# Role preparation of an RWKV-7 branch: the order of the key's factor against the gate copy, and of the norm's sums against the gate product

## The reference

```
r, k, v, wd, ad, gd = jnp.split(p, RWKV_SPLITS, axis=-1)
w_log = -jax.nn.softplus(-(w0 + jnp.tanh(wd) @ w_up)) - 0.5
decay = jnp.exp(-jnp.exp(w_log.astype(f32)))
a = jax.nn.sigmoid(a0 + ad @ a_up)
g = jax.nn.sigmoid(gd) @ g_up
kk = heads(k * k_k)
kk = kk / jnp.maximum(jnp.linalg.norm(kk, axis=-1, keepdims=True), 1e-12)
k = k * (1 + (a - 1) * k_a)
...
bonus = jnp.sum(r_h * k_h * r_k.astype(f32), axis=-1, keepdims=True) * v_h
```

## Time and profile before

| what | value |
|---|---|
| device time, three runs | 3651.9, 3652.07 and 3658.56 us, median 3652.07 |
| the profiled execution | 3661.2 us, its span 3659.3 us |
| busy over the whole span | PE 3353.8 us (92%), DVE 1444.1 (39%), ACT 994.7 (27%), POOL 121.3 (3%) |
| mean granted TensorE clock | 0.954 |

### The profile page before, as it was taken

How to read it: one execution, slowest core, us unless ns; L and a number is a source line. 1 busy time by engine, 2 the same in 40 slices (tenths; PEclk the granted TensorE clock), 3 DMA queues, 4 the chain that set the end, 5 groups by cost and what they waited for, 6 DMA issues and landing times. The chain is left out here.

```text
span 3659.3 us, 70478 instructions
## 1 busy us (share of the span) xinstructions
PE 3353.8 (92%) x28510; PEld 3114.1 (85%) x28510; DVE 1444.1 (39%) x2550; ACT 994.7 (27%) x1542; POOL 121.3 (3%) x126
## 2 busy tenths in 40 slices
PE   6999999999666888869979989999999999699898
PEld 5999999999545777769968789999999999588687
DVE  6566642222483666654435442222222222210433
ACT  5211123333472444431123331111111111211211
POOL 0000000000001222200000000000000000000000
PEclk8999999999776999979989989999999999899999
DMA  5233333433573343333334311111111110411433
GB/s 148 92 125 110 121 132 118 132 124 114 186 273 77 87 94 89 83 138 112 118 130 132 100 58 46 46 46 46 46 46 46 46 46 24 137 47 47 132 116 100
DMA packets 297472, 357.70 MB, mean 98 GB/s; under 512 B 133248, under 2 KB 245760, under 8 KB 285872
## 3 DMA queue, kind: packets, MB, share of 16 engines
q1 hardware_dynamic: 297392, 356.59, 30.8%
HBM read 221.52 MB, written 135.00 MB: 97 GB/s over the span
## 5 line engine op out<-in xcount | busy, mean ns | idle before, releaser
L2295 PE MATMUL psum<-h_hi,up_w_hi 128*128 128x344 f32 x2112 | 675.8, 320 | 15.3 <-DVE up_w_lo L2339 15.3
L2295 PE MATMUL psum<-h_lo,up_w_hi 128*128 128x344 f32 x2112 | 676.7, 320 | 0.0
L2295 PE MATMUL psum<-h_hi,up_w_lo 128*128 128x344 f32 x2112 | 674.4, 319 | 0.0
L434 PE MATMUL psum<-x_hi,proj_w_hi 128*128 128x344 f32 x1632 | 535.7, 328 | 8.5 <-DVE proj_w_lo L521 8.1
L434 PE MATMUL psum<-x_lo,proj_w_hi 128*128 128x344 f32 x1632 | 525.5, 322 | 0.0
L434 PE MATMUL psum<-x_hi,proj_w_lo 128*128 128x344 f32 x1632 | 524.3, 321 | 0.0
L2295 PEld LDWEIGHTS psum<-h_hi,up_w_hi 128*128 128x128 f32 x2112 | 397.5, 188 | 15.3 <-issue 15.3
L2295 PEld LDWEIGHTS psum<-h_hi,up_w_lo 128*128 128x128 f32 x2112 | 397.8, 188 | 0.0
L2295 PEld LDWEIGHTS psum<-h_lo,up_w_hi 128*128 128x128 f32 x2112 | 397.2, 188 | 0.0
L434 PEld LDWEIGHTS psum<-x_hi,proj_w_hi 128*128 128x128 f32 x1632 | 310.0, 190 | 10.3 <-issue 8.2
L2089 PE MATMUL psum<-down_w_hi,down_a_hi 128*128 128x512 f32 x704 | 278.8, 396 | 41.2 <-DVE down_w_lo L2209 30.6
(11 more groups left out here) (296 smaller groups left out, 5152.9 us busy)
## 6 DMA issues: line engine op xcount, KB each, us to landing
up_weight<-in_w_up_tiles SPq DMA_DIRECT2D x22, 1024.0 KB, 4.8
scratch_hidden<-up_hidden SPq DMA_DIRECT2D x22, 1024.0 KB, 3.9
down_a_raw<-scratch_hidden SPq DMA_DIRECT2D x32, 704.0 KB, 5.0
proj_area<-scratch_s_tab SPq DMA_DIRECT2D x32, 608.5 KB, 3.8
scratch_s_tab<-proj_area SPq DMA_DIRECT2D x16, 1089.0 KB, 4.3
proj_weight<-in_w_in_tiles SPq DMA_DIRECT2D x34, 512.0 KB, 4.1
scratch_gates<-proj_mixed SPq DMA_DIRECT2D x16, 1032.0 KB, 4.0
chunk_pre<-scratch_roles SPq DMA_DIRECT2D x128, 128.0 KB, 2.7
```

The lines of the kernel that those rows point to most:

```text
L434: mm = nc.tensor.matmul(psum[:, bank(v, n), 0:N_TOK], w[:, v, k, :], x[:, k, cols], start=(k == 0 and w is w_hi and x is x_hi), stop=(k == ...
L2295: mm = nc.tensor.matmul(psum[:, bank(u, part, n), 0:N_TOK], w[:, u, part, k, :], y[:, k, block_cols(n)], start=(k == 0 and w is w_hi and y ...
```

## The change

Two orders are exchanged. In TensorE's `early`, "norm" with its two waits now stands ahead of "g" with its wait. In ScalarE's `first_steps`, the factor with its two waits now stands ahead of the gate copy with its waits. No instruction is added or removed, and no buffer or semaphore is changed.

```diff
@@ early, TensorE
                 product("a", ups[64:128, 0, c], low[64:128, 0, t], n, a_summed)
-                pe.wait_ge(sig_ready, s + 1)
-                product("g", ups[:, 1, c], low[:, 1, t], n, g_summed)
                 pe.wait_ge(a_ready, s + 1)
                 pe.wait_ge(kk_squared, s + 1)
                 product("norm", heads[:], work[:, h], n, norm_summed)
+                pe.wait_ge(sig_ready, s + 1)
+                product("g", ups[:, 1, c], low[:, 1, t], n, g_summed)
@@ first_steps, ScalarE
                 A.activation(blocks(a[:, slot, 0:n]), banks_of("a", n), ACT.Sigmoid, ...).then_inc(a_ready, 1)
+                act.wait_ge(a_ready, s + 1)
+                if s >= SLOTS_3:
+                    act.wait_ge(bonus_stored[slot], 16 * (s // SLOTS_3))
+                A.activation(bonus[:, slot, 0:n], a[:, slot, 0:n], ACT.Identity, ...).then_inc(factor_ready, 1)
                 act.wait_ge(g_summed, s + 1)
                 if s >= 2:
                     act.wait_ge(gate_stored[h], 16 * (s // 2))
                 A.activation(blocks(gate[:, h, 0:n]), banks_of("g", n), ACT.Copy).then_inc(gate_ready, 1)
-                act.wait_ge(a_ready, s + 1)
-                if s >= SLOTS_3:
-                    act.wait_ge(bonus_stored[slot], 16 * (s // SLOTS_3))
-                A.activation(bonus[:, slot, 0:n], a[:, slot, 0:n], ACT.Identity, ...).then_inc(factor_ready, 1)
```

More of the change, by code:

```diff
@@ L901, in first_steps @@
                 A.activation(blocks(a[:, slot, 0:n]), banks_of("a", n), ACT.Sigmoid, bias=col("a0", j)).then_inc(a_ready, 1)
+                act.wait_ge(a_ready, s + 1)
+                if s >= SLOTS_3:
+                    act.wait_ge(bonus_stored[slot], 16 * (s // SLOTS_3))
+                A.activation(bonus[:, slot, 0:n], a[:, slot, 0:n], ACT.Identity, scale=col("k_a", j), bias=one_less[:, j:j + 1]).then_inc(factor_ready, 1)
                 act.wait_ge(g_summed, s + 1)
@@ L905, in first_steps @@
                 A.activation(blocks(gate[:, h, 0:n]), banks_of("g", n), ACT.Copy).then_inc(gate_ready, 1)
-                act.wait_ge(a_ready, s + 1)
-                if s >= SLOTS_3:
-                    act.wait_ge(bonus_stored[slot], 16 * (s // SLOTS_3))
-                A.activation(bonus[:, slot, 0:n], a[:, slot, 0:n], ACT.Identity, scale=col("k_a", j), bias=one_less[:, j:j + 1]).then_inc(factor_ready, 1)
             A.preload_act_table_set("sigmoid_and_others")
```

## The result

The changed kernel is slower: 3679.9 us in the median of five runs (3673.41 to 3684.64) against 3652.99 for the kernel before (five runs, 3651.9 to 3658.56). The ratio is 1.0072, with an interval of 1.0057 to 1.0087. That is +26.9 us between the medians, where +28.4 was forecast.

The account below looks back on a forecast made before the run. It took VectorE as nearest to a bound in role preparation, which passes its changes to the end. Six loops at +22.9 us and the first two units at +5.5 gave +28.4, 3680.5 us on 3652.07; range 3664 to 3690.

Parts of the forecast that it names:

- The factor's gain: VectorE's waits for the key's factor before L955, 3.69 and 4.00 us in units 3 and 5, would go.
- The series as the loop: From one L978 to the next, TensorE's and ScalarE's series bounds every unit: 19.98 us, +22.9 us over six loops.
- The clock: TensorE idles about 5 us; "a" and "norm" start at 1.2 GHz; the rise comes 4.5 us after "norm" begins.
- The head: First two units, before the first L978: a later gate copy costs +5.5 us, bounds +5.0 and +7.6.
- VectorE past unit 6: Past L978 of unit 6 no product of `early` is left and VectorE alone sets the pace: 0.
- Rival 1: Steady work raises TensorE's clock during "a"; "norm" and "g" run fast: +14.2 us, 3666.3; chance 0.12.
- Rival 2: TensorE's clock never falls, all loops 16.35 us: +4.0 us, 3656.1; chance 0.07.
- Rival 3: "norm" and "g" end early enough to hide ScalarE's exponentials; VectorE's factor waits go: −7.7 us, 3644.4; chance 0.06.
- Rival 4: Time gained at the factor and lost at the gate copy cancel: 3652 us; chance 0.02.
- rival 5: All loops with TensorE's products at 1.2 GHz: +37.6 us, 3689.7; chance 0.05.

Follow-up runs that it names:

- the second pair: Kernel before and changed kernel, each unaltered and run once more for its trace: 3648.2 and 3684.4 us.
- e7: Changed kernel with the gate product computed twice in a row: 3691.4 us (one run).
- e8: Changed kernel with the gate copy moved behind the exponentials (unit 0's stays) and the gate product computed twice: 3642.2 us (one run).
- e4: Changed kernel with the gate copy moved behind the previous unit's exponentials, unit 0's staying in place: 3644.5 us, ratio 0.9963 to the kernel before.
- e5: Changed kernel with more unread filler matmuls in TensorE's idle stretches than the first filler kernel had: 3656.5 us, ratio 0.9987 to the kernel before.
- e3: Changed kernel with matmuls whose sums nobody reads, filling TensorE's idle stretches: 3671.3 us, ratio 1.0029 to the kernel before.

## Why the prediction was right

The mechanism held, and the sum did too: +28.4 forecast, +26.9 measured. That the sum came so close is in part luck. In the first pair of traces the loops gave 24.9 us for 22.9, the head 2.7 for 5.5 and the end −0.6 for 0, and these misses cancel; the second pair has 24.7, 6.1 and 0, 30.9 in all. Part by part:

- *The factor's gain.* The waits before L955 fell from 15.7 to 1.7 us, as put. Nothing of it reached the end, since those units now wait further on. The wait for the norm's sums at L957, 1.3 us a loop, was not in the prediction; it adds nothing to its sum.
- *The series as the loop.* 19.98 us forecast, 20.31 measured on average. The terms of the loop from 1065.48 to 1085.97 are L981's end 2.45 (2.44 forecast), "a" 3.93 (3.71), sigmoid and handover 1.18 (1.17), "norm" and "g" 6.25 (5.93), copy, table load and handovers 2.35 (2.38), exponentials 4.30 (4.31). The terms with products at the low clock are what was mis-sized, by 0.5 us together. e7 and e8 show that "g" is in the series, e4 that the copy's place puts it there.
- *The clock.* The idle stretch was put at about 5 us and is 4.43 to 5.09; "a" and "norm" run at 0.50. The rise was put at 4.5 us after "norm" begins, a choice between 3.3 and never; it comes 4.0 to 5.1 us after in the six loops, and in the row at 1073.04 between 1077.9 and 1078.1, 4.9 to 5.1 on. One reading of the kernel before was too simple: the clock did not always fall ahead of the bonus product. For unit 0 it was 1.00 through the idle stretch from 979 to 983 and fell 0.1 us after the product had begun at 983.20, and so in units 2 and 4, 0.5 and 0.8 us after. In the changed kernel's six loops it fell in the idle stretch each time, which is what the sum needs.
- *What the low clock is worth.* e5 shows it: 20.3 against 16.2 us a loop, 24 us in six. With every loop at 16.24 the six would be 97.4 us, 0.4 above the kernel before. But two of that kernel's loops, of 18.7 and 19.0, have a low clock in their early products as well; against its short ones, 14.77, the series by itself costs 1.5 us. The loss takes both: e5 has the series without most of the low clock, e4 the low clock in part without the series, and each is rid of nearly all of it.
- *The head.* +5.5 was forecast; the two pairs of traces give +2.7 (41.3 − 38.6) and +6.1 (41.7 − 35.6), so its size is only bracketed. Unit 0's part was +1.6 in the first pair, for +2.0. Unit 1's was too high: from L884 to L920 it took 980.12 − 965.12 = 15.0 us, where 16.7 to 17.9 was put. "w" of unit 1 began at the high clock, and the rise in "norm" came 3.1 us after its start, earlier than the 3.3 that the prediction took for its end.
- *VectorE past unit 6:* put at 0; the last interval and what follows it measured 16.8 us for 17.4.

Rival 1, a rise during "a" by steady work of any kind, did not come about: "a" reads 0.50 to its end (1068.00 to 1071.80). The Trainium skill's page "TensorE: Matmul & The Clock Gate", "Part 1: The HAM clock gate", says that sustained activity releases the throttle. By that rule read plainly "norm" would have run at the high clock; the trace, with 0.50 until 4.9 us into it, does not show it, though 1.22 us of idling stand between "a" and "norm". The kernel before, with 0.50 in work without a gap (last section), disagrees more clearly. The rule's other half, that idling restores the throttle, agrees with the windows row at 1083.5, where the clock falls with TensorE idle. Rival 2 needed a clock that never falls, and e5 made one for most of the stage. Rival 3 needed the exponentials out of the copy's way, and e4 made that. Rival 4 falls with the interval, rival 5 with the rise that each loop does have, during "g".

What stays open: which part of its work decides when TensorE's clock rises, and why the rest of the span, the same code in all, lies between 3492 and 3506 us from one trace to the next (two traces of the same kernel differ by 9.8), so that e5 reads 0.9987 in device time with a stage 8.6 us longer than the first trace of before.

## What to carry to other kernels

An instruction that nobody needs soon is still expensive if it waits at the head of an in-order queue: ask what stands behind it, and for each exchange what it waits for afterwards. Here a copy that only a store and a later product wait for held back exponentials that had 0.33 us to spare in the row that the prediction read. Before putting one product ahead of another, see which of them ran under someone else's work; and where the engine between them loses its cover, price its products at the low clock, not at the one the old trace shows.

## What the runs showed of the hardware

TensorE being busy was not enough to bring or keep the high clock. In the kernel before it stayed at 0.50 through 12 us without a gap, over the bonus product of unit 1 and most of unit 3's:

```profile
998.50:1010.50 12.00, 12.00 (x31) 8.88 (x32) 10.41 (x9) 6.13 (x6) 0.00 (x0) 0.50 0.84 278
```

In e3 it fell in or just after "a" for units 2 to 5, 1.1 to 2.2 us after TensorE had come out of an idle stretch of only 0.9 to 2.0 us. In e5, whose stage has 492 matmul instructions for 320, it stayed at 1.00 from 990 to 1068. That work, which nobody reads, paid for itself: 18.5 us less in the stage than the changed kernel without it. Moving the copy did more, 38.3 us (e4).
